# YOCO decoder step on one core: cached keys turned by VectorE in 32x32 blocks, sample scores as eight 32x64-tile products in units of 1024 keys

## The reference, cut to what matters

```python
def latent_scores(q_lat, q_rope, c, kr):
    s = jnp.einsum('bqhc,bkc->bhqk', q_lat, c, preferred_element_type=jnp.float32)
    s = s + jnp.einsum('bqhr,bkr->bhqk', q_rope, kr, preferred_element_type=jnp.float32)
    return s * SM_SCALE

def sample_attention(q_lat, q_rope, past_c, past_kr, c, kr):
    s_past = latent_scores(q_lat, q_rope, past_c, past_kr)
    s_new = latent_scores(q_lat, q_rope, c, kr)          # masked to the lower triangle
    p = jax.nn.softmax(jnp.concatenate([s_past, s_new], axis=-1), axis=-1).astype(c.dtype)
    return (jnp.einsum('bhqk,bkc->bqhc', p[..., :P], past_c)
            + jnp.einsum('bhqk,bkc->bqhc', p[..., P:], c))

past_c = cache_kv_latent[page_table].reshape(DB, past_len, KV_LORA)     # 8 x 2048 x 512
past_kr = cache_k_rope[page_table].reshape(DB, past_len, QK_ROPE)       # 8 x 2048 x 64
```

## Time and profile before

| | us |
|---|---|
| median of 3 runs (1822.06 to 1822.7) | 1822.65 |
| the profiled execution, its own time | 1821.97 |
| its span, first to last instruction | 1820.2 |
| TensorE busy | 1735.6 (95%) |
| VectorE busy | 914.2 (50%) |
| ScalarE busy | 739.2 (41%) |
| GpSimd busy | 966.6 (53%) |

### The profile page before, as it was taken

One profiled execution on the slowest core, in us unless ns is written; L12 is line 12 of the kernel. 1 busy time (PEld: TensorE's weight loads), 2 busy tenths in 40 slices (PEclk: granted clock), 3 DMA queues, 4 the chain that ended last, 5 costly groups with the idle time before them and its releaser, 6 DMA issues. The chain is left out here.

```text
span 1820.2 us, 33590 instructions
## 1 busy us (share of the span) xinstructions
PE 1735.6 (95%) x12402; PEld 1578.6 (87%) x12402; DVE 914.2 (50%) x2228; ACT 739.2 (41%) x1463; POOL 966.6 (53%) x795
## 2 busy tenths in 40 slices
PE   7998899999999999899899899999989999999998
PEld 6997799998899999898776566666989999999988
DVE  5897799943423636673455444444261222222283
ACT  5565444454444543632233333333343222232342
POOL 4994799977799984753210000002655445554652
PEclk9998999999999999999999999999999999999999
DMA  7321455544355540323002155556412222322201
GB/s 205 106 87 56 121 180 163 163 152 139 117 162 162 164 148 26 120 66 117 13 0 79 52 157 156 156 155 207 139 63 77 70 92 92 92 69 69 93 24 53
DMA packets 183947, 198.58 MB, mean 109 GB/s; under 512 B 33065, under 2 KB 138115, under 8 KB 183826
## 3 DMA queue, kind: packets, MB, share of 16 engines
q1 hardware_dynamic: 179726, 194.28, 34.8%
q10 hardware_dynamic: 4100, 2.68, 0.5%
HBM read 192.14 MB, written 4.79 MB: 108 GB/s over the span
## 5 line engine op out<-in xcount | busy, mean ns | idle before, releaser
L1418 POOL TENSOR_TENSOR WL<-RAW,WH 128x1024 fp32r<-128x1024 f32 (+3 forms) x279 | 574.4, 2067 | 256.1 <-ACT WH L733 254.5
L2422 PE MATMUL bank<-AH,WH 128*128 128x288 f32 x2080 | 626.3, 301 | 30.6 <-DVE AL L1672 13.9
L2423 PE MATMUL bank<-AL,WH 128*128 128x288 f32 x2080 | 617.0, 297 | 0.0
L2424 PE MATMUL bank<-AH,WL 128*128 128x288 f32 x2080 | 616.7, 297 | 0.0
L2422 PEld LDWEIGHTS bank<-AH,WH 128*128 128x128 f32 x2080 | 394.6, 190 | 42.2 <-DVE AL L1672 16.7
L733 ACT ACTIVATE WH<-RAW 128x1024 fp32r<-128x1024 f32 (+1 forms) x281 | 292.0, 1045 | 264.9 <-PE bank L2424 264.4
L2423 PEld LDWEIGHTS bank<-AL,WH 128*128 128x128 f32 x2080 | 394.8, 190 | 0.7
L2424 PEld LDWEIGHTS bank<-AH,WL 128*128 128x128 f32 x2080 | 394.5, 190 | 0.0
L2422 PE MATMUL bank<-BH,WH 128*128 128x288 f32 (+1 forms) x1120 | 336.9, 301 | 13.7 <-DVE S L1721 4.1
L1416 POOL TENSOR_TENSOR WL<-RAW,WH 128x256 fp32r<-128x256 f32 (+2 forms) x135 | 119.2, 903 | 416.4 <-ACT WH L733 416.4
L2424 PE MATMUL bank<-BH,WL 128*128 128x288 f32 (+1 forms) x1120 | 333.4, 298 | 0.0
(11 more groups left out here) (298 smaller groups left out, 2131.6 us busy)
## 6 DMA issues: line engine op xcount, KB each, us to landing
RAW<-in_w_up SPq DMA_DIRECT2D x48, 1024.0 KB, 5.5
RAW<-in_w_down SPq DMA_DIRECT2D x48, 1024.0 KB, 5.1
RAW<-in_cache_kv_latent SPq DMA_DIRECT2D x128, 256.0 KB, 2.9
RAW<-in_conv_pw SPq DMA_DIRECT2D x16, 512.0 KB, 7.3
RAW<-in_conv_pw SPq DMA_DIRECT2D x8, 1024.0 KB, 5.2
RAW<-in_ple_gate SPq DMA_DIRECT2D x8, 1024.0 KB, 5.1
RAW<-in_cache_k_rope SPq DMA_DIRECT2D x128, 32.0 KB, 2.9
RAW<-in_w_o SPq DMA_DIRECT2D x4, 1024.0 KB, 6.1
```

Source lines behind the costliest of these rows:

```text
L1418: nc.gpsimd.tensor_tensor(dst, src, hi, ALU.subtract).then_inc(lo_done, 1)
L2422: nc.tensor.matmul(out, wh, xh, start=first, stop=False)
L2423: nc.tensor.matmul(out, wh, xl, start=False, stop=False)
L2424: return nc.tensor.matmul(out, wl, xh, start=False, stop=last)
```

## The change

- The 18 TensorE transposes of a slab go, with the copies from PSUM that followed them. VectorE turns the keys in 32x32 blocks, from SBUF to SBUF: `turn_pages` (128x2048 elements) and `turn_ropes` (128x256), each twice in a unit of 1024 keys.
- A block that is turned within its 32 partitions gives keys whose contraction is spread over four row groups. So the scores are products of 32 rows by 64 columns: 18 blocks by 4 row groups by 2 column halves, 144 products of 128 moving keys in a unit, each row group into a PSUM bank of its own. Softmax reads all four banks as one.
- The query has to lie in all four row groups: ScalarE issues 18 DMAs for each sample (`queries`) that copy it from `QLAT` and `QRS` into `Q4`.
- The unit is 1024 keys in place of 512, so softmax, the weights' copy and the running output are done twice a sample in place of four times. The TensorE, ScalarE and VectorE programs of the stage are written out, not looped.
- Four units are held: two in `RAW`, two in `WIDE`, which lies over `WH` and `WL`. So unit 0 is loaded as before, unit 1's latents when the last head's keys are done, its rotary part when the last head's scores are done, and so on. The split of the `wo` weights waits until units 13 and 14 are read.
- SyncE's loop runs over pairs of samples from sample 2 on. It still reads 16 page numbers and issues 32 DMAs for each sample, and samples 0 and 1 are written out ahead of it.
- The last head is reordered, with VectorE's first turns between its steps, and `sample_ropes` is done for two rows of blocks in place of one.

```diff
-            with sp.Fori(0, NS) as i:
+            pages_of(slice(0, 1))
+            sp.wait_ge(ones_set, 1)
+            sp.wait_ge(lo_done, PART0[DENSE0["kvh"] + 4])
+            sp.wait_ge(pe_read_raw, 2)
+            for s in range(2):
+                pages = [page(4 * s + q) for q in range(4)]
+                load_latents(0, s, pages)
+                load_ropes(0, s, pages)
+            sp.wait_ge(kvt_done, NH)
+            sp.wait_ge(v_mm, NH // 2)
+            for s in range(2):
+                load_latents(1, s, [page(8 + 4 * s + q) for q in range(4)])
+            sp.wait_ge(s_mm, 4 * NH)
+            for s in range(2):
+                load_ropes(1, s, [page(8 + 4 * s + q) for q in range(4)])
+            pages_of(slice(1, 2))
+            for s in range(2):
+                load_latents(2, s, [page(4 * s + q) for q in range(4)])
+            sp.wait_ge(pe_read_raw, 4)
+            sp.wait_ge(pv_mm, NH)
+            for s in range(2):
+                load_ropes(2, s, [page(4 * s + q) for q in range(4)])
+            for s in range(2):
+                pages = [page(8 + 4 * s + q) for q in range(4)]
+                load_latents(3, s, pages)
+                load_ropes(3, s, pages)
+            with sp.Fori(1, NS // 2) as i:
+                for e in range(2):
+                    pages_of(bass.ds(2 * i + e, 1))
+                    for k in (2 * e, 2 * e + 1):
+                        pages = [page(8 * (k % 2) + q) for q in range(8)]
+                        sp.wait_ge(unit_read, 4 * i + k - 3)
+                        sp.wait_ge(ones_set, 1)
+                        for s in range(2):
+                            load_latents(k, s, pages[4 * s:4 * s + 4])
+                            load_ropes(k, s, pages[4 * s:4 * s + 4])
...
+            def queries(i):
+
+                for m in range(4):
+                    for a in range(4):
+                        act.dma_start(Q4[i % 2][32 * a:32 * a + 32, 0:16].rearrange("p (c m) q -> p m c q", m=4)[:, m],
+                                      QLAT[32 * m:32 * m + 32, :, 64 * i:64 * i + 64]).then_inc(q4_in, 16)
+                for r in range(2):
+                    act.dma_start(Q4[i % 2][:, 16 + r], QRS[r][:, 64 * i:64 * i + 64]).then_inc(q4_in, 16)
...
+            def turn_pages(u, s):
+
+                dve.wait_ge(*half_landed(u, s))
+                if u >= 2:
+                    dve.wait_ge(score_mm, u - 1)
+                nc.vector.transpose(TURN[u % 2][:, 0:16, 128 * s:128 * s + 128].rearrange("p b (k j) -> p k b j", k=4),
+                                    half_pages(u, s).rearrange("p (k b j) -> p k b j", k=4, b=16)).then_inc(keys_turned, 1)
...
+            for u in range(1, UNITS2):
+                i, j = divmod(u, 2)
+                if u < UNITS2 - 1:
+                    turn_pages(u + 1, 0)
+                    turn_pages(u + 1, 1)
+                unit_top(u)
+                if u < UNITS2 - 1:
+                    turn_ropes(u + 1, 0)
+                    turn_ropes(u + 1, 1)
+                unit_sum(u)
...
+            def scores(u):
+
+                pe.wait_ge(keys_turned, CHUNKS * (u + 1))
+                for b in range(18):
+                    for a in range(4):
+                        rows32 = slice(32 * a, 32 * a + 32)
+                        for g in range(2):
+                            ins = nc.tensor.matmul(score_bank(u, a)[64 * g:64 * g + 64], Q4[u // 2 % 2][rows32, b, :],
+                                                   TURN[u % 2][rows32, b, P * g:P * g + P], start=b == 0, stop=b == 17)
+                ins.then_inc(score_mm, 1)
...
+            for u in range(1, UNITS2):
+                i, j = divmod(u, 2)
+                if u == 1:
+                    pe.wait_ge(csn_set, 1)
+                    pe.wait_ge(a_lo, A("o", 0, NH - 1))
+                scores(u)
+                if j and i:
+                    give(i - 1)
+                values(u - 1)
+                turn(u)
+                if j and i < NS - 1:
                     new_keys(i + 1)
```

More of the change, by code:

```diff
@@ L2253, in _ @@
+            for hd in range(NH - 1):
                 top(hd, 0)
@@ L2940, in _, with give @@
+            def give(i):
+                pe.wait_ge(out_done, OUTS + OUTS * i)
+                if i < NS - 1:
+                    pe.wait_ge(spt_c, 3 * (i + 1) + 2)
+                for c in range(4):
+                    ins = nc.tensor.matmul(give_bank(i)[:, c * 64:(c + 1) * 64], OUT[:, c * P:(c + 1) * P], JOIN,
+                                           start=True, stop=True)
+                ins.then_inc(out_mm, 1)
             rot(1, QR[:, 0, :])
@@ L2947, in _ @@
             pe.wait_ge(kv_staged, 10)
-            for hd in range(NH):
-                more, pair = hd < NH - 1, hd % 2 == 1 and hd < NH - 1
+            for hd in range(NH - 1):
+                pair = hd % 2 == 1
                 head_scores(hd, 0)
@@ L2960, in _ @@
                 head_uk(hd)
-                if not more:
-                    sample_ropes()
                 head_turn(hd, 1)
@@ L2966, in _ @@
                 head_scores(hd, 3)
-                if more:
-                    head_latent(hd)
+                head_latent(hd)
                 if pair:
@@ L3063, in give @@
-            def give(i):
-                pe.wait_ge(out_done, OUTS + OUTS * i)
-                pe.sem_inc(seen, 1)
-                for c in range(4):
-                    ins = nc.tensor.matmul(bank[7][:, c * 64:(c + 1) * 64], OUT[:, c * P:(c + 1) * P], JOIN, start=True,
-                                           stop=True)
-                ins.then_inc(out_mm, 1)
-            def sequence(i, first, last):
-                for j in range(4):
-                    scores(j, i)
-                    if j == 1 and not first:
-                        give(i - 1)
-                    if not (last and j == 3):
-                        keys(*((j + 1, i) if j < 3 else (0, i + 1)), range(5))
-                    if j:
-                        values(j - 1, i)
-                    elif not first:
-                        values(3, i - 1)
-                    turn(j, i)
-                if not last:
-                    new_keys(i + 1)
@@ new lines, in _ @@
+            head_out(hd - 1)
+            head_latent(hd)
+            sample_ropes()
+            head_turn(hd, 0)
+            head_scores(hd, 2)
+            head_turn(hd, 1)
+            head_scores(hd, 3)
+            head_turn(hd, 2)
+            pe.wait_ge(ql_used, NH)
+            pe.wait_ge(qrs_c, 2)
+            new_keys(0)
+            scores(0)
+            head_turn(hd, 3)
+            head_out(hd)
+            pe.wait_ge(pt_used, 4 * NH)
+            for c in range(4):
+                ins = nc.tensor.transpose(bank[6][0:TS, c * P:(c + 1) * P], CS[:, c, :], ident[:, :])
```

606 lines of the change are left out of this document (305 added, 301 removed).

## The result

The changed kernel takes 1836.8 us (median; 1834.4 to 1838.9) against 1822.7 for the kernel before in the same comparison: a ratio of 1.0076, with an interval of 1.006 to 1.0092. It is slower by 0.8%, where faster by 0.8% was forecast. The profiled execution takes 1836.9 us with a span of 1835.1, 14.9 us more than the span before. The output product starts at 1278.75 instead of 1264.72, so 14.0 of the 14.9 us come from the samples' attention and the head before it.

The account below looks back on a forecast made before the run. SyncE was to become the bound at 28.1 us a sample against 30.0; from 1015.5, 42.3 and 168.6 us plus the tail put the output product at 1250.8, a gain of 13.9 us: 1808.5 us, range 1799 to 1841.

Parts of the forecast that it names:

- 32 x 0.517 = 16.5: SyncE's samples loop: 32 DMA issues at 0.517 us take 16.5 us of a sample's forecast 28.1 us.
- Rival 3: ScalarE's issues hold up SyncE's: 0.1 us each, 1819.5 us, chance 0.08; or they exclude each other, 1846, chance 0.06.
- Issues that exclude each other: Stronger case of Rival 3, ScalarE against SyncE: 6.3 us a sample, 38 us in all, 1846 us; chance 0.06.
- TensorE's 20.6 us: Samples' attention: TensorE needs 2 x (4.5 scores + 3.7 values + 0.6 transposes) + 3.0 = 20.6 us a sample, in place of 30.
- Rival 1: Units' scores: the eight tiles don't run together; slower than before once scores pass 9.3 us, 1840 to 1936 us; chance 0.12.
- SyncE 28.1 against TensorE 20.6: Samples' attention: forecast us a sample for each engine, making SyncE the bound, against 30.0 before.
- ScalarE's issues, 0.33 to 0.35 us each: Query copies on ScalarE: 18 issues, 6.3 us behind the copy of a unit's weights, listed as costing nothing.
- Delay exponential 3 by some 5 us: Last head: ScalarE's query copies delay exponential 3 by some 5 us, covered by TensorE's first-unit scores.
- SyncE has 42 us ahead: Last head: SyncE still has 42 us of issues ahead, so the delay by ScalarE's copies costs nothing.
- rival 4: Samples' attention: SyncE is no bound, TensorE's 20.6 us a sample decides, stage ends 74 us earlier, 1748 us; chance 0.03.
- The tail: After the last cache load: it lands at 1228.8, then turn, softmax, scores and values lead to the output product at 1250.8.
- The sum: SyncE's start at 1015.5, 42.3 us ahead of the loop, 168.6 for six samples, then the tail: output product at 1250.8.

## Why the prediction was wrong

**The sign failed at "32 x 0.517 = 16.5".** With the excess of 3.0 us a sample these 32 issues took 19.5 us. From the first table of the loop to the last issue, 168.1 us were forecast (1057.8 to 1225.9) and 184.6 came (1064.2 to 1248.8). The excess of the issues in that time is 17.9 us, 13.6 of them from instruction loads and 4.3 from ScalarE. The gaps for tables and page numbers were right. The step took the spacing from a kernel whose TensorE ran a loop and whose ScalarE issued nothing there, and carried it over to one where both are otherwise. That the programs of the stage are written out, not looped, stood in the description of the change and was costed nowhere. The 1836.8 us lie inside the range of 1799 to 1841, but by luck: the range reached that far for tiles that don't run together, not for this.

**Rival 3 had a part of it.** Its +0.1 us for each of ScalarE's issues would be 1.8 us a sample; it was 0.7. Issues that exclude each other are ruled out: without the copies the excess of the issues of 0.36 to 0.8 us falls by 0.6 us a sample, and the time by 8 us and not by 38. The row it was read from gives less than was taken, too: 2.11 us for 4 holds the gaps between them, and four issues in a row take 1.88 undisturbed. The larger part, the instruction loads, had no rival at all.

**TensorE's 20.6 us.** Rival 1 falls: the eight tiles run together, 16.3 ns between matmuls, and 4.5 us for a unit (4.7 at that rate) is right while instructions last. But a unit took 6.1 to 10.5 us, and TensorE alone paces 29.6 us a sample, shown without the rotary loads. So "SyncE 28.1 against TensorE 20.6" was in truth 31.1 against 29.6. Even had the issues kept their spacing, the sample would by that run have been 29.6 at best, a gain of 0.4 us and not 1.9. So two terms of the forecast were wrong: SyncE's turned the gain into a loss, and TensorE's alone would have taken most of the gain away. Part of TensorE's time is the clock: the 15 values matmuls that take 4.0 us at full clock took 5.9 in the sample of the timeline above (1081.5), where the granted clock was 0.68 (the 1.2 GHz level up to 1085.3) after stops of 0.64 and 2.20 us, and it was 0.77 to 0.97 over the six samples. In the run without rotary loads it was 0.88.

**ScalarE's issues, 0.33 to 0.35 us each.** They took 0.62:

```profile
L1400 ACTq DMA_DIRECT2D S<-S x96: 608/624/1877, 1071.1 to 1241.3; - x96
```

The price came from two issues at the start that load a strip from memory; these move 32 partitions within SBUF. 18 cost 11.9 us in the last head, not 6.3. "Delay exponential 3 by some 5 us" was 11.1, "SyncE has 42 us ahead" was right in kind, but SyncE's wait for the last `head_out` (forecast as over at 1030) lasted until 1041.8. The stretch from 1017.3 to the loop's first table took 46.9 us for 42.3. That these copies are a third bound near 25 us a sample was not in the prediction either; it would have capped the gain of a faster SyncE, and puts rival 4's 20.6 us a sample out of reach as the kernel stands.

**The tail.** From the last issue to the output product 30.0 us came for 24.9. The last half was there 5.0 us after its issue started, not 2.9 (2.1 us), and the last unit's scores took 7.5 us for 4.5 (3.0 us), with stalls of 1.21 and 1.39.

**The sum.** Start +1.8, prologue +4.6, loop +16.5, tail +5.1: 28.0 us. The output product was forecast at 1250.8 and came at 1278.75.

**What was right.** VectorE's turn: 2.31 us for 2.3. SyncE is a bound, waits for no score, and reads its page numbers at the forecast price. The `wo` split and the transfers cost nothing to speak of: behind the stage only 0.9 us more are lost. That 1808.5 lies beside the 1806.9 and 1803.9 us which came with the instructions spread and the rotary loads moved is luck: the forecast has SyncE at 28.1 us a sample with all its loads, and these runs have TensorE at 25.2 and 25.1 and SyncE with half of them.

## What to carry over

A price that was read from a loop holds for the loop: before unrolling or splitting into smaller tiles, count the engine's instructions per microsecond against the size and the latency of its instruction loads, and mix short instructions with long ones. Where one engine is taken off a bound, price the next one in the new kernel's conditions and look for a third; where two are level, expect single edits to give little and test them in pairs. DMAs that one engine issues are not free for another engine that has no slack.

## What the hardware did that I had not expected

- Matmuls of 32 rows by 64 columns with 128 moving float32 columns ran 16.3 ns apart on average (128 in 2.09 us), 8 tiles in turn. The Trainium skill ("TensorE: Matmul & The Clock Gate", the section on 56 against 53.3 ns) has them never under about 25 ns, and says nothing there of tiles; this case's rows are below that, and the measurement decides. In the trace's regular stretches the eight start 6 to 11 ns apart, then some 60 ns pass before the next eight, and a round takes 110 ns (the median; 131 on average in the 2.09 us). Two tiles of the kernel before, with as many columns (line 3111, rows 9), take 109 ns a round, so six more tiles cost next to nothing. With 256 columns and four tiles a round takes 216 ns, twice as long for half the tiles, and that is why the run with half the instructions had 55.6 ns. So the time of a round went with the columns, not with the number of tiles, in these three shapes. The kernel before already showed starts 6 to 7 ns apart, in the pairs of lines 3059 and 3111.
- TensorE's code arrives in packets of 16 KB. At 256 instructions in 2.1 us it outran them and stood for 0.4 to 2.5 us at their boundaries; the program before, at 440 instructions in 30 us, never did, in a loop or written out. Over all runs 156 such stops lie in the scores, and each ends 0.9 to 1.7 us after the end of a packet.
- An issue of SyncE that lies over such a packet can take 0.5 to 1.7 us longer. Of the 178 cache issues over 0.8 us in all 17 profiles 176 lie over one, and the other two over a packet of 8 KB on a second instruction queue. Not every packet does it: of 30 packets in the changed kernel's loop 17 lay over an issue and 14 of these lengthened it, but in the run of nine blocks without rotary loads and copies it was none of 5. What decides is open; that the two share the DMA rings was not tested.
- ScalarE's issues of copies within SBUF take 0.62 us, GpSimd's of the same rotary loads 0.53, SyncE's 0.33.
